# A gate vector moved from VectorE's dot products to TensorE's matrix products, inside the first layer's attention

## The chip, the cores and the metric

The kernel runs on one core of a Trainium2 chip, in one launch. The metric is the device time of the whole kernel in microseconds (us), the median of several runs. A profiled execution gives the trace from which all rows below are read. Times in the trace count from the start of its span.

## The reference, cut to what matters

The model is two blocks of two layers each over 256 tokens of width 1024. Each layer of the first block begins with a vector `mod` that is computed from a conditioning vector `c` and cut into six parts of 1024 numbers:

```python
mod = silu(c) @ w_ada[l] + b_ada[l]                      # w_ada[l]: 1024 x 6144
sh1, sc1, g1, sh2, sc2, g2 = split(mod, 6)
h = rms_norm(x, norm_g[l, 0]) * (1 + sc1) + sh1
...                                                      # h @ w_in, three mixers: 12 softmax heads, 4 linear ones
mix = concat([o_a, o_b, o_c]) @ w_out[l]
x = x + g1 * mix                                         # g1 is the mixer gate
h = rms_norm(x, norm_g[l, 1]) * (1 + sc2) + sh2
x = x + g2 * conv_ffn(h, ...)
```

The change is about `g1` of the first layer: 1024 numbers, each a dot product of `silu(c)` with a column of `w_ada[0]`, plus a bias.

## The kernel before, in words

Activations lie transposed: 1024 features as 8 chunks of 128 partitions, 256 tokens along the free side. All weights come from HBM in units of 512 KB; SyncE (SP) issues their loads in a written-out order into a ring of 8 slots, and waits for a slot to be freed before it issues the next, so that everything behind a waiting load waits too.

The conditioning vectors need no matrix product before: `w_ada` is stored so that a "row" n is a 128 x 1024 tile whose partition p holds the column of `w_ada` for output feature 128n + p. VectorE multiplies the tile by `silu(c)` (the same on all partitions, in `crow`) and sums along the free side, which gives 128 outputs (`do_ada`, L1810; one such operation is called a dot here). There are 48 rows in a layer: 0 to 15 for the first shift and scale, 16 to 23 for `g1`, 24 to 39 for the second shift and scale, 40 to 47 for `g2`. Rows from 16 on pass through four slots of their own; row n is loaded (L679) once the dot of row n - 4 is done (semaphore `ada_used`). Written-out lists spread the dots over stages in which VectorE was thought free: `ADA_UNITS` gives how many come at each step of the attention, `ADA_OUT` how many at each part of the output projection. `mods` (L1818) then adds the bias.

The attention of the first layer has 12 units (a pair of heads by 128 queries) in a software pipeline over steps. At step s TensorE multiplies the scores of unit s, turns the probabilities of unit s - 3 (four transposes, L921), and multiplies the values of unit s - 4 into one of four PSUM banks (a "job" of this unit). Before the last, it multiplies seven times by zeros (`keep_warm`, L776; bf16, 256 columns), whose results are overwritten. VectorE at step s does its dots, then the maximum of the scores of unit s, the reciprocals of unit s - 1 and the copy of the result of unit s - 5 (L1912), which frees its bank for the job two later. ScalarE exponentiates and copies the turned probabilities out of PSUM; GpSimd scales the probabilities (L1751). Everything waits in order on its own engine.

Then comes the output projection: three banks of two tiles each, then two halves (`last_tiles`), with VectorE adding `g1` times each bank to `x` (`residual`, L1842) between dots, ScalarE squaring the new `x` and TensorE summing the squares for the next norm. Of the eight weight units of this projection (20 to 27), SP issues six before rows 20 to 29 of `w_ada`, two between rows 29 and 30, and the next stage's units between the later rows:

```python
ADA_LOADS = {RING + 6: 4, U_IN + 5: 10, U_IN + 7: 4, U_IN + 8: 2, U_IN + 9: 2, U_IN + 10: 2}
ADA_UNITS, ADA_OUT = [[0] * 4 + [1] * 6 + [2] * 2, [0] * NATT], [(5, 5, 4, 0), (0, 0, 0, 0)]
```

Of the kernel before, what the change touches and what calls it, by code (L numbers as in the profile page):

```python
# [30 lines left out]
RING = 8  # L31
ADA_RING = 4
ADA = 6 * DC
N_CMP, CMP_LEN, CMP_STRIDE = 15, 32, 16
NSA_H, REL_BUCKETS, REL_MAX = 16, 32, 128
PH, NK, TOPK = 8, 128, 16
# [26 lines left out]
def columns():  # L63

    at, n = {}, 0
    for l in range(DEPTH):
        for name, k in (("ng1", DC), ("ng2", DC), ("cw0", 2 * FC), ("cw1", 2 * FC), ("cw2", 2 * FC), ("cb", 2 * FC),
                        ("aq", 1), ("ak", 1), ("cq", 1), ("ck", 1), ("bo", 1), ("lb", 4)):
            at[name, l] = n
            n += k  # L70
    for l in range(2 * DEPTH):
        at["bada", l] = n
        n += ADA
    for name, k in (("png", 4 * DC), ("fcw", 12), ("fq", 1), ("fk", 1), ("bf", 1),
                    ("nq", 1), ("nkc_lo", 1), ("nkc_hi", 1), ("nks", 1), ("nkw", 1),
                    ("bgate", 48), ("pos", 2 * CMP_LEN)):
        at[name] = n
        n += k
    return at, n
# [97 lines left out]
def lay_out(x):  # L177
# [37 lines left out]
    put("bgate", np.broadcast_to(g["odd_b_gate_2"][0], (P, 48)))  # L215
    pos = g["odd_cmp_pos_2"][0]
    put("pos", np.concatenate([dup(pos[0].T), dup(pos[1].T)], 1))
    out["params"] = par
    out["consts"] = constants()
    out["mixer_consts"] = mixer_constants()  # L220
# [2 lines left out]
    out["rel"] = np.ascontiguousarray(table[distance_rows()].transpose(0, 2, 1)).reshape(P, NSA_H * T)  # L223
    out["c_rows"] = np.ascontiguousarray(np.stack([np.broadcast_to(g["c"][0], (P, D)), np.broadcast_to(g["c_2"][0], (P, D))], 1))
    out["ada"] = np.stack([w.T.reshape(ADA, P, D) for w in (*g["w_ada"], *g["ada_w_2"])])

    units = []
    for l in range(DEPTH):
# [74 lines left out]
def build(nc, io, out):  # L303
# [7 lines left out]
    with ctx:  # L311
# [310 lines left out]
        ADA_TURNS = [[24] + [2] * FC + [8, 8, 8, 0], [0] + [2] * 16 + [3] * 6 + [6, 6, 6, 0]]  # L622
        ADA_FOX = (9, 18, 23, 29)
        ADA_LOADS = {RING + 6: 4, U_IN + 5: 10, U_IN + 7: 4, U_IN + 8: 2, U_IN + 9: 2, U_IN + 10: 2}
        ADA_UNITS, ADA_OUT = [[0] * 4 + [1] * 6 + [2] * 2, [0] * NATT], [(5, 5, 4, 0), (0, 0, 0, 0)]
        EARLY = 2 * DEPTH * ADA
        assert EARLY - 16 - sum(map(sum, ADA_TURNS)) == 16
        FIRST = CONST["ones"][1]
# [34 lines left out]
        def _(sp):  # L663
# [6 lines left out]
            def load_ada(k):  # L670

                for _ in range(min(k, EARLY - ada_n[0])):
                    n = ada_n[0]
                    if n >= 16 + ADA_RING:
                        sp.wait_ge(sem("ada_used"), n - ADA_RING + 1)
                    elif n >= 16:
                        sp.wait_ge(sem("ada_used"), 16)
                    arrived = sem(f"ada_first{n // 2}") if n < 16 else sem(f"ada_in{n % ADA_RING}")
                    sp.dma_start(ada_slot(n), io["ada"][n // ADA, ada_row(n)]).then_inc(arrived, 16)  # L679
                    ada_n[0] += 1  # L680
# [64 lines left out]
        def _(pe):  # L745
# [27 lines left out]
            def keep_warm(to, n):  # L773

                for _ in range(n):
                    nc.tensor.matmul(to, zero_b[:, 0:P], zero_b, start=True, stop=True)  # L776

            def norm_stat(o):
                b = open_job("norm", o, 0)
# [109 lines left out]
                        mm(out_[:, h, t], kk[side, h, s * P:(s + 1) * P], qq[side, h, t * P:(t + 1) * P],  # L889
                           signal=sem("lev_filled") if h == 3 and t == 1 else None)  # L890

            def attention(name, us, u0, beside={}, warm={}, warm_values=0):
                n, jobs = len(us), 0
                for step in range(n + 4):
                    if step in beside:
# [28 lines left out]
                    if 0 <= step - 4 < n:  # L924
                        u, un = u0 + step - 4, us[step - 4]
                        nc_ = keys_of(un) // P
                        if un.first:
                            j = (*name, jobs)
                            jobs += 1
                            ob = open_job(*j)  # L930
                            keep_warm(ob[:, 0:T], warm_values)
                        pe.wait_ge(*freed("pt", *name, step - 4))
                        if un.pre is not None:
                            mm(ob[:, 0:P], un.pre[0], un.pre[1], True, False)
                        for c in range(nc_):
                            for hh in range(2):
                                side = slice(hh * HD, (hh + 1) * HD)
                                end = hh and c == nc_ - 1
                                mm(ob[side, 0:P], un.v[:, c, side], pt[:, u % 2, hh, c],
                                   un.first and un.pre is None and c == 0, c == nc_ - 1 and un.last,  # L940
                                   None if not end else filled(*j)[0] if un.last else sem("pv_mid"))

            pe.wait_ge(sem("ones_in"), 16)
            for l in range(DEPTH):
# [34 lines left out]
                def outputs_B():  # L979

                    b = open_job("ob", l, 0)
                    for cc in range(2):
                        for t in range(TT):
# [5 lines left out]

                attention(("att", l), units_of(l), l * NATT,   # L990
                          {1: lambda: pe.wait_ge(sem("lev_freed"), NLEV * (l + 1)), 2: outputs_B, NATT: lambda: stat("statB", l, 1, "sqB", l + 1),
                           6: lambda: pe.wait_ge(sem("qkC"), l + 1)}, *WARM_ATT[l])

                mixed = {c: [freed("att", l, 2 * (c if c < 3 else c - 2) + t) for t in range(TT)] for c in (0, 1, 2, 5, 6, 7)}
                mixed[3] = [(sem("mixB"), l + 1)]
# [315 lines left out]
        def _(act):  # L1311
# [3 lines left out]
            def wait(*sv):  # L1315
                act.wait_ge(*sv)
# [212 lines left out]
            wait(sem("c_in"), 16)  # L1529
            seq(A(crow[:, 0], crow[:, 0], ACT.Silu), "c_silu")  # L1530
            wait(sem("params_in"), 16)

            wait(sem("x_in"), 16)
            for l in range(DEPTH):
# [256 lines left out]
        def _(dve):  # L1791
# [3 lines left out]
            def wait(*sv):  # L1795
                dve.wait_ge(*sv)
# [2 lines left out]

            def do_ada(k):  # L1800
                for _ in range(min(k, EARLY - ada_n[0])):
                    n = ada_n[0]
                    if n < 16:
                        wait(sem(f"ada_first{n // 2}"), 32)
                    else:
                        wait(sem(f"ada_in{n % ADA_RING}"), 16 * ((n - 16) // ADA_RING + 1))
                    if n == DEPTH * ADA:
                        wait(sem("c_silu"), 2)
                    l, ch = n // ADA, ada_row(n)
                    seq(V.tensor_tensor_reduce(out=junk, in0=ada_slot(n), in1=crow[:, l // DEPTH], scale=1.0,  # L1810
                                               scalar=0.0, op0=ALU.mult, op1=ALU.add,
                                               accum_out=mod[:, l, ch // DC, ch % DC:ch % DC + 1]), "ada_used")
                    ada_n[0] += 1
# [60 lines left out]
                for c in range(DC):  # L1874
                    scale(1, c, "h_scaled")

            def attention(name, us, u0, projections=None, beside={}):
                n, jobs = len(us), 0
                projections = projections or [0] * n
                for step in range(n + 5):  # L1880
# [27 lines left out]
                    if 0 <= step - 5 < n and us[step - 5].last:  # L1908
                        j = (*name, jobs)
                        jobs += 1  # L1910
                        wait(*filled(*j))
                        seq(V.tensor_copy(us[step - 5].out, bank_of(*j)[:, 0:P]), *freed(*j))  # L1912

            V.memset(epsc[:, :], EPS).then_inc(sem("eps_set"), 1)
# [30 lines left out]
            for l in range(DEPTH):  # L1945
# [100 lines left out]
                def norm_B():  # L2046
# [2 lines left out]
                    seq(V.tensor_tensor(mixT[:, 3:5], oB, gB, ALU.mult), "mixB")  # L2049

                attention(("att", l), units_of(l), l * NATT, ADA_UNITS[l],
                          {0: lambda: None if l == 0 else roots_C(3), 1: lambda: roots_C(0), 2: lambda: roots_C(1), 3: lambda: roots_C(2), 4: norm_C, NATT + 2: lambda: roots_B(0), NATT + 3: lambda: roots_B(1)})
                norm_B()
                if l == 0:
                    mods(0, 2, 3)
                residual(2 * l + 1, ("out", l), l, 2, ADA_OUT[l], None if l else lambda: mods(0, 3, 5))
                for k in range(FC):
                    g = l * FC + k
# [341 lines left out]
```

## Time and profile before

| what | us |
|---|---|
| median of 3 runs (lowest, highest) | 2473.94 (2468.49, 2475.46) |
| profiled execution, its own time | 2471.28 |
| span of its trace | 2469.5 |
| TensorE matmul busy | 2407.2 |
| VectorE busy | 1612.8 |
| ScalarE busy | 847.6 |
| GpSimd busy | 298.9 |

The profiled execution is 2.66 us below the median. Its own time is 1.78 us more than the span, which is what lies around the traced instructions. The stage in question, from the start of the attention to the end of the output projection, is less than 90 us of the span (121 to 209 us).

### The profile page before, as it was taken

Reading aid. Unit: us, or ns where it says so; the run is one execution under the profiler, and the core shown is the slowest. Engines: PE = TensorE matmul, PEld = TensorE weight load, DVE = VectorE, ACT = ScalarE, POOL = GpSimd, SP = SyncE. Lnnn points to the kernel's source line nnn. Section 1 sums busy time; section 2 is a strip of 40 time slices with the busy share of each in tenths; the row PEclk is TensorE's granted clock in tenths of the full one; section 3 lists DMA queues with packets and bytes.
Section 4 is the critical chain, followed back from the end, with each engine's and each line's share of the span. In section 5 each row is a group of like instructions: output and inputs, shape, how many; then the busy total and the mean of one; then the engine's idle time right before and its main releaser. Section 6 shows DMA issues by size and latency. Waiting matters only on the chain.

```text
span 2469.5 us, 46042 instructions
## 1 busy us (share of the span) xinstructions
PE 2407.2 (97%) x17350; PEld 2234.2 (90%) x17350; DVE 1612.8 (65%) x3756; ACT 847.6 (34%) x2183; POOL 298.9 (12%) x386
## 2 busy tenths in 40 slices
PE   7989999999999999999999999999899999999998
PEld 6868889878888987999999999989599999999998
DVE  6886665574666273795888883325639958888634
ACT  2542120443110113223665540022622246655300
POOL 1030110010110001010111121100401101111110
PEclk9999999999999999999999999999999999999999
DMA  8447888314889562699999999954038989999997
GB/s 321 158 166 280 305 291 331 129 59 147 312 302 360 198 245 78 224 413 347 401 408 402 407 405 414 394 193 162 1 129 316 414 325 409 407 396 413 406 413 294
DMA packets 171489, 727.06 MB, mean 294 GB/s; under 512 B 19152, under 2 KB 19664, under 8 KB 146384
## 3 DMA queue, kind: packets, MB, share of 16 engines
q1 hardware_dynamic: 142992, 521.76, 56.4%
q0 software_dynamic: 27648, 201.34, 20.1%
q10 hardware_dynamic: 704, 2.10, 0.4%
q8 instruction: 82, 1.34, 0.2%
q14 instruction: 63, 0.52, 0.1%
HBM read 721.97 MB, written 1.05 MB: 293 GB/s over the span
## 4 chain that ended last, share of the span: by engine, by line
PE 87%; DVE 6%; DMA 3%; ACT 2%; issue 2%; POOL 0%; SPq 0%; DVEq 0%; ACTq 0%
PE banks L749 36%; PE lev L1152 23%; PE banks L1098 21%; DMA ring<-in_peer_u 2%; PE lev L749 2%; PE banks L1079 1%; PE lev L1079 1%; PE banks L865 1%; PE banks L921 1%; DMA extra<-in_ada 1%; DVE arena L1965 1%; DVE arena L2031 0%; ACT arena L1423 0%; DVE arena L1991 0%; DVE arena L1894 0%
## 5 line engine op out<-in xcount | busy, mean ns | idle before, releaser
L749 PE MATMUL banks<-hT,ring 128*128 128x256 f32 (+1 forms) x2832 | 584.5, 367 | 4.8 <-ACT hT L1332 3.2
L1098 PE MATMUL banks<-hT,ring 128*128 128x160 f32 x4096 | 579.4, 301 | 3.6 <-DMA ring<-in_peer_u 3.3
L749 PEld LDWEIGHTS banks<-hT,ring 128*128 128x128 f32 x2832 | 513.1, 190 | 72.5 <-ACT hT L1332 5.0
L1152 PE MATMUL lev<-arena,ring 128*128 x4096 | 576.8, 301 | 0.0
L1098 PEld LDWEIGHTS banks<-hT,ring 128*128 128x128 f32 x4096 | 559.2, 190 | 5.3 <-DMA ring<-in_peer_u 1.9
L1152 PEld LDWEIGHTS lev<-arena,ring 128*128 128x128 f32 x4096 | 559.0, 190 | 0.2
L1781 POOL DMA_INDIRECT arena<-in_peer_rows,keysb x192 | 184.9, 963 | 1131.5 <-DVE consts L2192 675.0
L749 PE MATMUL banks<-arena,ring 128*128 128x256 f32 (+2 forms) x1648 | 284.9, 334 | 0.7 <-DVE arena L2049 0.7
L749 PEld LDWEIGHTS banks<-arena,ring 128*128 128x128 f32 x1648 | 259.1, 192 | 25.4 <-DVE arena L2049 1.1
L2239 DVE SCALAR_TENSOR_TENSOR extra<-consts,chT 128x192 bf16<-128x192 f32 x640 | 223.8, 409 | 17.8 <-ACT arena L1471 17.6
L2204 DVE CUSTOM_DVE_ANT_0 arena<-arena 128x1024 f32<-128x1024 f32 x64 | 78.2, 1222 | 165.2 <-DMA arena<-in_peer_rows,keysb 165.1
L2192 DVE SCALAR_TENSOR_TENSOR consts<-arena,extra,consts 128x1024 f32<-128x1024 f32 x128 | 164.1, 1282 | 6.4 <-ACT extra L1482 6.4
L2204 DVE CUSTOM_DVE_ANT_0 arena<-arena,consts 128x1024 f32<-128x1024 f32 x128 | 155.4, 1214 | 0.3
L1810 DVE CUSTOM_DVE_ANT_0 arena<-arena 128x1024 f32<-128x1024 f32 x104 | 130.1, 1251 | 35.1 <-DMA arena<-in_ada 31.5
L1471 ACT ACTIVATE arena<-banks 128x320 f32<-128x320 f32 x128 | 55.9, 437 | 276.2 <-PE banks L1098 255.0
L1491 ACT ACTIVATE std<-consts,chT 128x128 bf16<-128x128 f32 x320 | 102.0, 389 | 76.4 <-PE banks L1079 60.0
L1480 ACT ACTIVATE extra<-extra 128x1 f32<-128x1 f32 x192 | 37.2, 194 | 264.5 <-DVE extra L2204 264.5
L1491 ACT ACTIVATE rstd<-consts,chT 128x128 bf16<-128x128 f32 x320 | 102.0, 389 | 73.3 <-PE banks L1079 54.5
L1618 ACT ACTIVATE arena<-banks,params 128x256 f32<-128x256 f32 x88 | 44.8, 559 | 237.0 <-PE banks L749 237.0
L1810 DVE CUSTOM_DVE_ANT_0 arena<-extra,arena 128x1024 f32<-128x1024 f32 x88 | 109.0, 1238 | 21.6 <-DMA extra<-in_ada 18.9
L1751 POOL TENSOR_SCALAR arena<-arena,rinv 128x256 f32<-128x256 f32 (+1 forms) x128 | 64.1, 513 | 417.8 <-DVE rinv L1904 258.2
L2065 DVE SCALAR_TENSOR_TENSOR arena<-banks,params,arena 128x255 f32<-128x255 f32 x88 | 42.5, 483 | 101.0 <-ACT arena L1618 99.4
(286 smaller groups left out, 2284.3 us busy)
## 6 DMA issues: line engine op xcount, KB each, us to landing
ring<-in_peer_u SPq DMA_DIRECT2D x256, 512.0 KB
ring<-in_peer_v SPq DMA_DIRECT2D x256, 512.0 KB
ring<-in_stream_first SPq DMA_DIRECT2D x188, 512.0 KB
arena<-in_ada SPq DMA_DIRECT2D x104, 512.0 KB, 5.4
extra<-in_ada SPq DMA_DIRECT2D x88, 512.0 KB, 5.3
ring<-in_stream_nsa SPq DMA_DIRECT2D x45, 512.0 KB
ring<-in_stream_fox SPq DMA_DIRECT2D x41, 512.0 KB
arena<-in_peer_rows,keysb POOLq DMA_INDIRECT x192
```

The source lines that it names most:

```text
L749: ins = nc.tensor.matmul(o, lhsT, rhs, start=start, stop=stop, **kw)
L1079: ins = nc.tensor.matmul(gate_banks[half][k % 2][:, t * 256:t * 256 + HALF], hot_r[:, k % 2, t], hot_c[:, k % 2, t, i], start=i == 0, stop ...
L1098: ins = nc.tensor.matmul(banks[k // 2 % 4][:, (k % 2) * ND:(k % 2 + 1) * ND], ring[:, u % RING, c], hT[:, c, NS:T], start=c == 0, stop=c = ...
L1152: ins = nc.tensor.matmul(lev[c // 4][:, (c % 4) * T + NS:(c % 4 + 1) * T], ring[:, u % RING, c], a[:, bass.ds(g, 1), k], start=False, stop ...
L1471: A(acts_g[:, g, 2 * k:2 * k + 2], banks[k][:, 0:2 * ND].rearrange("p (a t) -> p a t", a=2), ACT.Gelu_apprx_tanh).then_inc(sem("act_freed" ...
L1491: A(dist[q % 2][:, t], iota, ACT.Abs, bias=chT[:, 0, 4 * q + t:4 * q + t + 1])\
L1751: G.tensor_scalar(x, x, rinv[:, u % 4, hh:hh + 1], 1.0, ALU.mult, ALU.mult).then_inc(sem("probs_ready"), 1)
L1781: G.indirect_dma_start(out=rows[:, n % ROWS], out_offset=None, in_=io["peer_rows"], in_offset=bass.IndirectOffsetOnAxis(ap=eid[:, k:k + 1] ...
L1810: seq(V.tensor_tensor_reduce(out=junk, in0=ada_slot(n), in1=crow[:, l // DEPTH], scale=1.0, scalar=0.0, op0=ALU.mult, op1=ALU.add, accum_o ...
L2192: V.scalar_tensor_tensor(out=y, in0=rows[:, n % ROWS, D:2 * D], scalar=row_act[:, k:k + 1], in1=y, op0=ALU.mult, op1=ALU.add).then_inc(sem ...
L2204: V.tensor_tensor_reduce(out=u, in0=u, in1=xn[i], scale=1.0, scalar=0.0, op0=ALU.mult, op1=ALU.add, accum_out=row_act[:, k:k + 1]).then_in ...
L2239: ins = V.scalar_tensor_tensor(out=hot_c[:, q % 2, t], in0=iota[:, half * HALF:(half + 1) * HALF].unsqueeze(1).broadcast_to([P, PARTS, HALF]),
```

## The change

Rows 16 to 23 are no longer dots. They are stored so that each 128 x 128 block of a row's tile is a weight for TensorE (input features on the partitions, output features along the free side). `silu(c)` is also kept as `ccol`, one column per chunk and each column twice, computed by a small operation of ScalarE at the start; it adds 16 columns to the loaded parameters. In the jobs of units 0 to 5 the seven products by zeros are replaced by `gate_products`: two rows in jobs 0 and 1, one in jobs 2 to 5, each row 8 matrix products (f32, 128 x 128 weights, 2 moving columns) that accumulate into two spare columns of the job's bank. VectorE adds the bias to each row's column, before the copy of this job, with one operation on 128 x 1. The jobs of units 6 to 11 keep their zeros.

VectorE's dots in the attention go from 10 (one at steps 4 to 9, two at 10 and 11) to 4 (one at steps 8 to 11), those in the output projection from 14 to 12; the call of `mods` for the gate is gone. SP's order of loads is the same, but rows 20 to 27 now wait for TensorE's use of rows 16 to 23, and rows 28 on for the dots of rows 24 on.

```diff
+GATE_ROWS = range(2 * DC, 3 * DC)
...
+    put("ccol", np.repeat(ch(g["c"][0]), 2, 1))
...
+    for n in GATE_ROWS:
+        out["ada"][0, n] = g["w_ada"][0][:, n * P:(n + 1) * P].reshape(DC, P, P).transpose(1, 0, 2).reshape(P, D)
...
-        ADA_UNITS, ADA_OUT = [[0] * 4 + [1] * 6 + [2] * 2, [0] * NATT], [(5, 5, 4, 0), (0, 0, 0, 0)]
+        ADA_UNITS, ADA_OUT = [[0] * 8 + [1] * 4, [0] * NATT], [(4, 4, 4, 0), (0, 0, 0, 0)]
+        GATE_JOBS = [{0: (16, 17), 1: (18, 19), 2: (20,), 3: (21,), 4: (22,), 5: (23,)}, {}]
+        ccol = col("ccol", None, 0, 2 * DC).rearrange("p (c a) -> p c a", a=2)
...
-                    if n >= 16 + ADA_RING:
-                        sp.wait_ge(sem("ada_used"), n - ADA_RING + 1)
+                    if n >= 24 + ADA_RING:
+                        sp.wait_ge(sem("ada_used"), n - ADA_RING + 1 - DC)
+                    elif n >= 16 + ADA_RING:
+                        sp.wait_ge(sem("gate_rows"), n - ADA_RING - 16 + 1)
...
+            def gate_products(b, rows):
+
+                for i, n in enumerate(rows):
+                    if n == GATE_ROWS[0]:
+                        pe.wait_ge(sem("c_col"), 1)
+                    pe.wait_ge(sem(f"ada_in{n % ADA_RING}"), 16 * ((n - 16) // ADA_RING + 1))
+                    for c in range(DC):
+                        mm(b[:, T + 2 * i:T + 2 * i + 2], ada_slot(n)[:, c * P:(c + 1) * P], ccol[:, c], c == 0, c == DC - 1,
+                           sem("gate_rows") if c == DC - 1 else None)
...
-                            keep_warm(ob[:, 0:T], warm_values)
+                            if jobs - 1 in gates:
+                                gate_products(ob, gates[jobs - 1])
+                            else:
+                                keep_warm(ob[:, 0:T], warm_values)
...
+            A(ccol, ccol, ACT.Silu).then_inc(sem("c_col"), 1)
...
+                    if ada_n[0] == GATE_ROWS[0]:
+                        ada_n[0] += DC
...
+                        for i, r in enumerate(gates.get(jobs - 1, ())):
+                            r -= GATE_ROWS[0]
+                            seq(V.tensor_tensor(mod[:, 0, 2, r:r + 1], bank_of(*j)[:, T + 2 * i:T + 2 * i + 1],
+                                                col("bada", 0, GATE_ROWS[0] + r), ALU.add))
...
-                if l == 0:
-                    mods(0, 2, 3)
```

## Rows read from the trace of the kernel before

**Rows 1.** The page: the chain that ended last by engine, and one group.
```profile
PE 87%; DVE 6%; DMA 3%; ACT 2%; issue 2%; POOL 0%; SPq 0%; DVEq 0%; ACTq 0%
...
L1480 ACT ACTIVATE extra<-extra 128x1 f32<-128x1 f32 x192 | 37.2, 194 | 264.5 <-DVE extra L2204 264.5
```

**Rows 2.** Timeline of VectorE, attention: start us, us, instruction, [idle before].
```profile
149.91 1.28 DVE L1810 CUSTOM_DVE_ANT_0 arena<-arena 128x1024 f32<-128x1024 f32 x1
...
152.69 1.28 DVE L1810 CUSTOM_DVE_ANT_0 arena<-extra,arena 128x1024 f32<-128x1024 f32 x1
...
154.02 1.37 DVE L1810 CUSTOM_DVE_ANT_0 arena<-extra,arena 128x1024 f32<-128x1024 f32 x1
```

**Rows 3.** Timeline of TensorE, attention; an f32 product is two passes, counted singly.
```profile
134.32 0.93 PE L776 MATMUL banks<-zero 128*128 128x256 bf16 x7
...
143.55 0.70 PE L749 MATMUL lev<-arena 64*128 64x256 f32 x4
144.18 0.66 PE L921 MATMUL banks<-consts,arena 128*128 128x128 f32 x4
144.68 0.93 PE L776 MATMUL banks<-zero 128*128 128x256 bf16 x7
145.53 0.66 PE L749 MATMUL banks<-arena 128*64 128x128 f32 x8
146.12 0.70 PE L749 MATMUL lev<-arena 64*128 64x256 f32 x4
...
156.92 0.94 PE L776 MATMUL banks<-zero 128*128 128x256 bf16 x7 [1.46 <-DVE arena L1912]
...
161.21 0.63 PE L921 MATMUL banks<-consts,arena 128*128 128x128 f32 x4 [1.71 <-DVE arena L1912]
```

**Rows 4.** Timeline of TensorE, output projection.
```profile
169.22 24.56 PE L749 MATMUL banks<-arena,ring 128*128 128x256 f32 x128
...
196.80 0.75 PE L749 MATMUL banks<-arena,consts 128*128 128x128 f32 x4 [2.13 <-ACT arena L1323]
197.35 3.58 PE L749 MATMUL banks<-arena,ring 128*128 128x128 f32 x16
...
207.22 1.95 PE L749 MATMUL banks<-hT,ring 128*128 128x128 f32 x16
```

**Rows 5.** Timeline of TensorE, the last sums of the experts, 32 columns moving.
```profile
1616.18 1.87 PE L1166 MATMUL lev<-folds,arena 128*128 128x32 f32 x16
1617.88 1.69 PE L776 MATMUL banks<-zero 128*128 128x256 bf16 x14
```

**Rows 6.** TensorE by line and form: xcount, busy us, mean ns, idle before.
```profile
L749 PE MATMUL banks<-arena 128*128 128x30 f32 x32 | 3.7, 271 | 0.0
...
L1138 PE MATMUL lev<-zero 128*128 128x2 bf16 x8 | 0.5, 163 | 1.2 <-ACT arena L1471 1.2
```

**Rows 7.** Windows: stretch, length, then busy time by engine, TensorE's granted clock, DMA.
```profile
124.00:126.00 2.00, 1.37 (x12) 0.70 (x8) 1.93 (x3) 0.36 (x1) 0.00 (x0) 0.92 0.03 8
126.00:128.00 2.00, 2.00 (x13) 1.25 (x14) 1.95 (x2) 0.66 (x4) 0.00 (x0) 0.50 0.00 0
...
198.00:200.00 2.00, 2.00 (x11) 2.00 (x11) 0.00 (x0) 0.00 (x0) 0.00 (x0) 0.50 0.00 0
...
1714.00:1716.00 2.00, 2.00 (x22) 2.00 (x20) 2.00 (x1) 0.00 (x0) 0.00 (x0) 1.00 0.00 0
```

**Rows 8.** Timeline of VectorE, output projection.
```profile
171.25 0.17 DVE L1818 TENSOR_TENSOR mod<-mod,params 128x8 f32<-128x8 f32 x1
...
192.62 1.23 DVE L1810 CUSTOM_DVE_ANT_0 arena<-extra,arena 128x1024 f32<-128x1024 f32 x1 [1.35 <-DMA extra<-in_ada]
...
195.15 0.88 DVE L1842 SCALAR_TENSOR_TENSOR xT<-banks,mod,xT 128x256 f32<-128x256 f32 x2
```

**Rows 9.** Loads of `w_ada` rows, 120 to 200 us, from issue to landing.
```profile
DMA to landing us min/median/max: 3.0/4.6/6.8
```

**Rows 10.** SP's queue in the same stage: issues merged by line.
```profile
172.71 1.60 SPq L679 DMA_DIRECT2D extra<-in_ada  x2
```

More of the change, by code:

```diff
@@ L75, in columns @@
                     ("nq", 1), ("nkc_lo", 1), ("nkc_hi", 1), ("nks", 1), ("nkw", 1),
-                    ("bgate", 48), ("pos", 2 * CMP_LEN)):
+                    ("bgate", 48), ("pos", 2 * CMP_LEN), ("ccol", 2 * DC)):
         at[name] = n
@@ L890, in level, with attention @@
                            signal=sem("lev_filled") if h == 3 and t == 1 else None)
-            def attention(name, us, u0, beside={}, warm={}, warm_values=0):
+            def attention(name, us, u0, beside={}, warm={}, warm_values=0, gates={}):
                 n, jobs = len(us), 0
@@ L991, in _ @@
                           {1: lambda: pe.wait_ge(sem("lev_freed"), NLEV * (l + 1)), 2: outputs_B, NATT: lambda: stat("statB", l, 1, "sqB", l + 1),
-                           6: lambda: pe.wait_ge(sem("qkC"), l + 1)}, *WARM_ATT[l])
+                           6: lambda: pe.wait_ge(sem("qkC"), l + 1)}, *WARM_ATT[l], GATE_JOBS[l])
                 mixed = {c: [freed("att", l, 2 * (c if c < 3 else c - 2) + t) for t in range(TT)] for c in (0, 1, 2, 5, 6, 7)}
@@ L1875, in residual, with attention @@
                     scale(1, c, "h_scaled")
-            def attention(name, us, u0, projections=None, beside={}):
+            def attention(name, us, u0, projections=None, beside={}, gates={}):
                 n, jobs = len(us), 0
@@ L2051, in _ @@
                 attention(("att", l), units_of(l), l * NATT, ADA_UNITS[l],
-                          {0: lambda: None if l == 0 else roots_C(3), 1: lambda: roots_C(0), 2: lambda: roots_C(1), 3: lambda: roots_C(2), 4: norm_C, NATT + 2: lambda: roots_B(0), NATT + 3: lambda: roots_B(1)})
+                          {0: lambda: None if l == 0 else roots_C(3), 1: lambda: roots_C(0), 2: lambda: roots_C(1), 3: lambda: roots_C(2), 4: norm_C, NATT + 2: lambda: roots_B(0), NATT + 3: lambda: roots_B(1)}, GATE_JOBS[l])
                 norm_B()
-                if l == 0:
-                    mods(0, 2, 3)
                 residual(2 * l + 1, ("out", l), l, 2, ADA_OUT[l], None if l else lambda: mods(0, 3, 5))
```

## The prediction

> **What bounds the kernel now.** I read the page's chain first: 87% of the span is TensorE, 6% VectorE [rows 1]. So a dot that leaves VectorE is worth something only where VectorE is on the chain, and a product that TensorE gains costs its whole time wherever TensorE is. I therefore went to the attention of the first layer, in the timelines of both engines. VectorE runs there without a gap: with one dot a step takes 2.78 us (149.91 to 152.69), of which the dot is 1.28 [rows 2]; a second dot adds 1.33 (152.69 to 154.02), which makes about 4.1. TensorE, when nothing holds it, needs 2.57 us for a step (143.55 to 146.12): scores 0.63, transposes 0.50, seven zeros 0.85, values 0.59 [rows 3]. In the steps with one dot the two are nearly equal. In the two steps with two dots TensorE waits, 1.46 and 1.71 us [rows 3], and these two waits are about all that ten dots cost here. The output projection starts at 169.22 [rows 4]. I call this moment T0.
>
> Behind T0 TensorE works through the projection, then stands still for 2.13 us at 194.7 to 196.8, waiting for ScalarE's squares of the new x [rows 4]. These wait for VectorE's add at 195.15, which came late because the dots before it waited for their rows from HBM (1.35 us for the last pair) [rows 8]. After this wait the clock was granted at half: 0.50 in 198 to 200 us [rows 7]. Sixteen passes took 3.58 us there, and the like sixteen 1.95 us at full clock [rows 4]: 1.63 us lost.
>
> **What the gate costs on TensorE.** No product with 2 columns and f32 weights is in the trace. The nearest have 32 columns: sixteen passes, the number of one row (8 products of two passes), from 1616.18 to 1617.88, 1.70 us, 0.106 a pass [rows 5]. With 30 columns it is 3.7 us for 32, 0.116 a pass [rows 6]. Since 32 columns are no faster than 128 (1.95 less the overlap of the last), the weights set the pace, and I take 1.70 us for a row. Below, the bound is the bf16 product with 2 columns, 0.5 us for eight, 0.062 each [rows 6], or 1.0 us a row; but f32 weights are twice the bytes, and I stay at 1.70. Above it is 1.86 with the 30-column figure. The seven zeros that go cost 0.85. So blocks with two rows gain 2.55 us, those with one 0.85.
>
> The Trainium skill (TensorE: Matmul & The Clock Gate, section Back-to-back issue gap) gives about 25 ns from start to start for products of 1 to 64 columns; by that a row would be 0.4 us and cheaper than the zeros. The 32-column row has four times this, and I go by the row.
>
> **T0 at full clock.** A step now is scores, transposes and values, 1.72 us, and the products. Job 0 begins at 134.32 as before [rows 3]; two steps of 5.12 and four of 3.42 bring job 6 to 158.2. From its zeros on: 1.44 for zeros and values of job 6, 2.57 for step 11, then 1.94, 1.94, 1.94 and 1.44 for steps 12 to 15, 0.9 for the statistic of the linear heads in step 12 (two passes of 512 columns, each twice a pass of 256 columns at 24.56 us for 128 passes of which 32 are half as wide [rows 4], 0.22), and an estimate of 0.5 for the wait for its square root, together 12.7. T0 is 170.9, or 1.7 later than before. In place of a kernel held by two double dots stands one held by 13.6 us of gate products (8 x 1.70) where 5.1 us of zeros were.
>
> Is VectorE hidden then? With one dot its step is 2.78, against 3.42 of TensorE in steps 8 and 9 and 2.57 in 10 and 11; it starts these with steps 4 to 7 without dots behind it, so it follows TensorE's scores by about 2 us at the end, and the copy of job 5 is there when the zeros of job 7 need it. The eight bias adds are 0.2 each by the like operation on 128 x 8 [rows 8], 1.6 us spread over steps in which VectorE waits; without this cover they would cost that much. The bias call of 0.2 that goes was off TensorE's path too.
>
> SP's queue: row 20 is issued once row 16 is used, at about 136, and a load lands in 3.0 us at least, 4.6 at the median [rows 9]; job 2 wants it at 144.6. Rows 24 to 27 follow the single blocks, from about 146.3 in steps of 3.42, and land 3.0 later, at 149.3, when VectorE asks; even the median 4.6 delays a dot by 1.6 us at a place with 2 us to spare. Behind them in the queue stand rows 28 and 29 and weight units 26 and 27, which are wanted only at the end of the projection.
>
> **The projection.** VectorE has 12 dots, not 14, and SP issues rows 30 and 31 at once behind unit 27, where row 30 stood at 172.71, T0 + 3.5 [rows 10], since the dots that they wait for are done. Each later row is issued about 2.5 us nearer to T0. Chained through, the last dot ends near T0 + 20.5, and the third bank is only there at T0 + 21 (96 passes of 0.22). So the add is done by T0 + 22, not at 196.0, T0 + 26.8; TensorE wants the squares at 194.7, T0 + 25.4. The wait goes (-2.1) and with it the half clock behind it (-1.6). What is late next is TensorE itself. The small silu of `ccol` adds about 0.2 at the start, where ScalarE leads to the first norm; such operations take 194 ns [rows 1].
>
> At full clock all this gives 1.7 + 0.2 - 2.1 - 1.6 = -1.8 us.
>
> **The clock.** The zeros stand there for the clock, and what replaces them moves 2 columns a pass where they moved 256. Before the fall at 125.7 TensorE was busy 1.37 of 2 us, partly on half of its rows (64 of 128), and then had 0.50 [rows 7]. The only long stretch of thin products, 3.7 us with 30 columns [rows 6], kept 1.00 in 1714 to 1716 [rows 7]; but it has 15 times the columns and dense work on both sides. Neither row settles what 3.4 us of 2-column products do. I take the clock to fall: a half-clock stretch like the one in [rows 4] loses 1.63 us. The gates of job 1 at half clock take 6.8 us, about twice the 3.58 of that row, and I add one more among jobs 2 to 5, whose steps are half gates: 3 x 1.63 = 4.9.
>
> The Trainium skill (the same page, section Why this matters for your kernels) asks only that TensorE have no long idle gap between bursts. The gates leave none, so by this rule the clock stays. The fall at 125.7 came with TensorE idle for only 0.63 of the 2 us around it [rows 7], so the trace doesn't bear it out fully.
>
> The forecast is -1.8 + 4.9 = +3.1 us: 2474.3 on the profiled 2471.28, and 2477 on the median 2473.94.
>
> **Rivals.**
> A. The clock stays at 1.00: a busy engine is enough. For it speaks 1714 to 1716. The sum is -1.8, 2472.1.
> B. The clock is at half through most of the six blocks. Each single step then has 3.4 us of gates and up to 3.4 of other work (1.72 doubled), and the clock falls again as soon as it has come back. With ten stretches it is -1.8 + 16.3 = +14.5, 2488.4. It is slower beyond what can be measured from the sixth stretch on (-1.8 + 6 x 1.63 = 8.0). Against it: the four single steps have dense work in between, and such work gave the clock back in the projection, where the sixteen passes from 207.22 run at full pace again [rows 4].
> C. The wait in the projection stays, since ten rows still come through there and full bandwidth is shared with the weight units. Then the 3.7 us aren't recovered: +6.8, 2480.7. Against it: some 3 us of slack.
> D. The 2-column passes run at 0.062. A row is 1.0 and costs 0.15 more than the zeros; the steps are 3.7 twice and 2.7 four times, T0 is near 165.4, or about 166 (an estimate) with VectorE's four dots, and the sum is about -3.2 + 0.2 - 3.7 = -6.7, 2467.2. Against it: [rows 5].
> That the dots don't leave VectorE is not possible by the diff.
>
> **How the numbers follow.** Chances: forecast (one to five stretches) 0.45, A 0.28, B 0.12, C 0.08, D 0.07. Within 0.3% (7.4 us, about what a measurement of this kernel tells from no change) lie A, C and nearly all of the forecast, and half of D: 0.79. Slower holds B and 0.03 of forecast and C: 0.15. Faster holds the rest of D and what I have missed: 0.06. The range is 2467 to 2487: D's edge below, all of the forecast's own 2473 to 2480, A and C, and half of B; under 0.2 is left out.
>
> **What would show it.** Right: gate rows of 16 passes with 1.70 us from start to start; TensorE without waits in steps 4 to 11; T0 between 171 and 177; two to four stretches with a granted clock of 0.50 between 135 and 165; no idle time before the norm's sums at T0 + 25 and 1.00 behind it. Wrong: a row under 1.2 or over 2 us; TensorE waiting for rows 20 to 23 or for VectorE's copies; a wait of 2 us left in the projection; the clock at 1.00 throughout, or at half to 170.

## The result, and the profile after

The changed kernel takes 2483.28 us (median of 9 runs, 2478.01 to 2488.80) against 2471.94 us for the kernel before (9 runs): a ratio of 1.0047, with a 95% interval of 1.0035 to 1.0058, or about 11 us more. The forecast was 2477 in a range of 2467 to 2487. The time lies in the range and on the side of the forecast, but at more than three times its +3.1, and in the class "slower by over 0.3%", which had a chance of 0.15. It is above the 2473 to 2480 of the forecast's own case: the range held it because it took in half of rival B.

The profiled execution took 2488.80 us, the longest of the nine, with a span of 2486.9 against 2469.5. The timeline of TensorE in the attention of the first layer, where [rows 3] stood:

```profile
133.27 3.63 PE L757 MATMUL banks<-params,arena 128*128 128x2 f32 x32
136.83 0.66 PE L757 MATMUL banks<-arena 128*64 128x128 f32 x8
...
139.41 6.83 PE L757 MATMUL banks<-params,extra 128*128 128x2 f32 x32
146.17 1.12 PE L757 MATMUL banks<-arena 128*64 128x128 f32 x8
147.22 1.23 PE L757 MATMUL lev<-arena 64*128 64x256 f32 x4
148.37 1.11 PE L939 MATMUL banks<-consts,arena 128*128 128x128 f32 x4
149.28 3.41 PE L757 MATMUL banks<-params,arena 128*128 128x2 f32 x16
152.62 1.12 PE L757 MATMUL banks<-arena 128*64 128x128 f32 x8
```

The first two rows of the gate take 3.56 us together (133.27 to 136.83). Behind them the values still run at full pace (0.59 to the next start), but from the scores at 137.42 on everything takes about twice as long: the two rows of job 1 take 6.76 us, one row 3.34, and the scores, transposes and values around them are as slow. A single step takes 6.45 us (149.28 to the like place at 155.73) where 3.42 was reckoned. The windows say why (stretch, length, busy us of TensorE, its weight loads, VectorE, ScalarE, GpSimd, then TensorE's granted clock, the DMA engines' share and GB/s):

```profile
134.00:137.00 3.00, 3.00 (x29) 2.98 (x31) 2.41 (x4) 2.79 (x9) 2.31 (x3) 1.00 0.25 76
138.00:178.00 40.00, 40.00 (x201) 33.40 (x199) 14.05 (x49) 9.42 (x31) 9.74 (x12) 0.50 0.36 123
178.00:180.00 2.00, 2.00 (x15) 1.36 (x15) 0.97 (x5) 0.52 (x3) 0.00 (x0) 0.88 0.46 186
```

For 40 us on end TensorE was busy without a break and had half its clock (1.2 GHz). It came back only after the first job that has zeros again (175.09). The kernel before had 1.00 from 130 to 190 us; around this stage it fell twice, each time for some 3 us: before 130 us, and behind the wait in the projection [rows 7]. VectorE is busy 14 of the 40 us: it now waits for scores, 8.09 us before the maximum of unit 6.

```profile
148.59 0.42 DVE L1918 CUSTOM_DVE_ANT_0 arena<-lev,arena 128x256 f32<-128x256 f32 x1 [8.09 <-PE lev L757]
```

The projection, where [rows 4] and [rows 8] stood, on TensorE and then on VectorE:

```profile
188.86 24.56 PE L757 MATMUL banks<-arena,ring 128*128 128x256 f32 x128
213.25 1.06 PE L757 MATMUL banks<-arena,consts 128*128 128x128 f32 x8
214.57 0.71 PE L757 MATMUL banks<-arena,consts 128*128 128x128 f32 x4 [0.26 <-ACT arena L1344]
215.12 1.95 PE L757 MATMUL banks<-arena,ring 128*128 128x128 f32 x16
```

```profile
194.71 1.23 DVE L1834 CUSTOM_DVE_ANT_0 arena<-extra,arena 128x1024 f32<-128x1024 f32 x1 [1.33 <-DMA extra<-in_ada]
...
212.92 0.88 DVE L1866 SCALAR_TENSOR_TENSOR xT<-banks,mod,xT 128x256 f32<-128x256 f32 x2
```

The wait of 2.13 us is 0.26 now, and the sixteen passes behind it take 1.95 us where they took 3.58. Two lengths can be worked out from such timelines for every kernel: A, from the first product of job 0 to T0 (the start of the projection), and B, from T0 to the place in the next stage where TensorE waits 0.48 us for ScalarE's hT. Before, A is 34.90 us (134.32 to 169.22) and B is 40.43 (to 209.65). After, A is 55.59 and B is 36.93. Their sum grew by 17.2 us, and the span by 17.4: all of the loss is here, 20.7 lost in the attention and 3.5 given back in the projection.

The nine executions differ in how long the clock is at half. The one of 2478.01 us has a mean granted clock of 0.991 over a span of 2475.9, the profiled one 0.987 over 2486.9: worked out, 45 and 65 us at half clock in the whole kernel, against 25 us at the 0.995 of the kernel before, each to within some 2.5 us, since the mean clock is given to 0.001. The profiled execution is the worst case of the nine, not a middle one.

### The profile page after: what moved, and what is told of

Read it like the earlier page. It is cut to its first block, busy times and chain, and to the rows that moved or that the text cites. A ratio compares the mean times of both kernels' runs of the same rounds, so it can differ in the third digit from the quotient of the medians.

```text
span 2486.9 us, 46204 instructions
## 1 busy us (share of the span) xinstructions
PE 2432.2 (98%) x17436; PEld 2258.6 (91%) x17436; DVE 1603.1 (64%) x3747; ACT 848.1 (34%) x2184; POOL 296.6 (12%) x386
## 4 chain that ended last, share of the span: by engine, by line
PE 88%; DVE 6%; DMA 3%; ACT 2%; issue 1%; POOL 0%; SPq 0%; DVEq 0%; ACTq 0%
PE banks L757 37%; PE lev L1173 23%; PE banks L1119 21%; PE lev L757 2%; DMA ring<-in_peer_u 2%; PE banks L1100 1%; PE lev L1100 1%; PE banks L883 1%; PE banks L939 1%; DMA extra<-in_ada 1%; DVE arena L1993 1%; DVE arena L2059 0%; ACT arena L1444 0%; PE banks L784 0%; DVE arena L2019 0%
## 5 line engine op out<-in xcount | busy, mean ns | idle before, releaser
L2230 DVE CUSTOM_DVE_ANT_0 arena<-arena 128x1024 f32<-128x1024 f32 x64 | 78.2, 1222 | 166.7 <-DMA arena<-in_peer_rows,keysb 166.7
L1834 DVE CUSTOM_DVE_ANT_0 arena<-arena 128x1024 f32<-128x1024 f32 x100 | 124.7, 1247 | 37.8 <-DMA arena<-in_ada 34.3
L1834 DVE CUSTOM_DVE_ANT_0 arena<-extra,arena 128x1024 f32<-128x1024 f32 x84 | 103.8, 1236 | 22.1 <-DMA extra<-in_ada 19.6
```

The source lines that it names most:

```text
L2230: V.tensor_tensor_reduce(out=u, in0=u, in1=xn[i], scale=1.0, scalar=0.0, op0=ALU.mult, op1=ALU.add, accum_out=row_act[:, k:k + 1]).then_in ...
```

## The experiments

In the text below "over" and "under" are against the kernel before on the same chip. In the edits, what is not shown is as in the changed kernel unless it says otherwise.

**1. As many columns as the weights' pace gives for nothing: 128.**

```diff
-    mm(b[:, T + 2 * i:T + 2 * i + 2], ada_slot(n)[:, c * P:(c + 1) * P], ccol[:, c], ...
+    mm(b[:, T + 128 * i:T + 128 * i + 128], ada_slot(n)[:, c * P:(c + 1) * P], ccol[:, c, 0:1].broadcast_to([P, 128]), ...
```

VectorE's bias add reads column 128i of the spare ones instead of 2i.

> The changed kernel with 128 moving columns in each gate product instead of 2 (the same column 128 times), nothing else. Theory: the half clock of 137 to 178 us comes from what the gate products stream, 2 columns a pass, while the weights alone set their pace. Then a row still takes about 1.8 us, TensorE's clock stays at 1.00 from 134 us to the projection, the projection starts near 171 instead of 188.9, and the time is 1 to 3 us under the kernel before (ratio 0.999). Rival: it is the chain of long weight-bound stretches itself, whatever it streams. Then the clock is 0.50 here too and the time is that of the changed kernel, ratio 1.004.

Measured: 2469.17 us against 2473.33, ratio 0.9984 (0.9975 to 0.9992), 4.2 us under. The windows of the attention and of the projection, columns as above:

```profile
134.00:172.00 38.00, 37.53 (x335) 29.98 (x336) 23.49 (x69) 20.34 (x55) 10.28 (x20) 1.00 0.45 153
172.00:210.00 38.00, 37.32 (x237) 34.10 (x236) 26.57 (x57) 9.91 (x24) 0.00 (x0) 1.00 0.72 278
```

and two of its rows in the timeline, with the start of the projection:

```profile
134.35 3.74 PE L757 MATMUL banks<-params,arena 128*128 128x128 f32 x32
138.01 0.66 PE L757 MATMUL banks<-arena 128*64 128x128 f32 x8
...
145.11 1.95 PE L757 MATMUL banks<-params,arena 128*128 128x128 f32 x16
146.99 0.66 PE L757 MATMUL banks<-arena 128*64 128x128 f32 x8
...
172.42 24.56 PE L757 MATMUL banks<-arena,ring 128*128 128x256 f32 x128
```

The same products with 64 times the columns cost 3.66 us for two rows instead of 3.56, the clock is 1.00 throughout, and A is 38.07. Nothing else differs from the changed kernel but the column that the bias add reads, so the half clock there is caused by how little the products stream, not by their number, their weights or any wait that the change moved. The rival falls.

**2. 32 columns.** The same edit with 32 in place of 128.

> The changed kernel with 32 moving columns in each gate product. If streaming matters, this stands between 2 and 128: a row takes 1.7 us at full clock, and half-clock stretches are fewer than in the changed kernel; time 0 to 8 us over the kernel before. If streaming doesn't matter, it is the changed kernel's time, 11 us over.

Measured: 2483.93 us, ratio 1.0042 (1.0027 to 1.0056), 10.6 us over: no better than 2 columns. The profiled execution had the whole block at half clock:

```profile
134.00:137.00 3.00, 3.00 (x28) 2.99 (x27) 2.55 (x5) 2.79 (x8) 2.14 (x3) 1.00 0.18 40
138.00:178.00 40.00, 40.00 (x199) 33.21 (x195) 14.05 (x49) 9.61 (x31) 9.74 (x12) 0.50 0.36 119
```

I had expected something in between. Taken alone the run would have fitted the rival, that streaming doesn't matter; beside experiment 1 it says that this kernel loses the clock with 32 columns as it does with 2.

**3. Thin products in the kernel before.** In the kernel before, the zeros of jobs 0 to 5 give way to as many products of 2 columns as the change has; their results are overwritten. The dots stay.

```diff
-    keep_warm(ob[:, 0:T], warm_values)
+    if name == ("att", 0) and jobs - 1 < 6:
+        for c in range(16 if jobs - 1 < 2 else 8):
+            nc.tensor.matmul(ob[:, T:T + 2], ident, ones[:, 0:2], start=True, stop=True)
+    else:
+        keep_warm(ob[:, 0:T], warm_values)
```

> The kernel before, with all its dots on VectorE, where only the seven products by zeros of jobs 0 to 5 are replaced by as many thin ones as the change has (16 f32 products of 2 columns in jobs 0 and 1, 8 in jobs 2 to 5; their results are overwritten). Theory: the clock falls to 0.50 as in the changed kernel, and the loss is at least the changed kernel's: 11 to 20 us over the kernel before, since the wait in the projection stays or shrinks only with the later start. Rival: the fall is due to something else that the change moved (waits for rows, the copies on VectorE); then the clock stays at 1.00 and the time is 2 to 5 us over.

Measured: 2483.87 us, ratio 1.0047 (1.0030 to 1.0065), 10.5 us over. This is the changed kernel's loss, without its change of the dots. In the profiled execution the clock came back twice on the way, at about 156 us, only to be lost again before 160, and at about 166, both times with nothing but thin rows, scores, transposes and values since the fall:

```profile
139.00:156.00 17.00, 17.00 (x86) 15.00 (x85) 6.73 (x18) 4.34 (x16) 5.75 (x6) 0.50 0.38 123
156.00:160.00 4.00, 4.00 (x37) 3.48 (x35) 2.67 (x9) 1.63 (x6) 1.90 (x2) 0.93 0.19 38
160.00:166.00 6.00, 6.00 (x31) 5.00 (x32) 2.54 (x9) 1.50 (x6) 1.89 (x2) 0.50 0.45 152
```

```profile
156.15 1.89 PE L933 MATMUL banks<-consts 128*128 128x2 f32 x16
...
159.70 3.42 PE L933 MATMUL banks<-consts 128*128 128x2 f32 x16
...
166.16 1.99 PE L933 MATMUL banks<-consts 128*128 128x2 f32 x16
```

A is 49.23 (134.23 to 183.46), and TensorE still waits 2.86 us in the projection. What lets the clock come back in one execution and not in another I haven't tested; the same kind of difference stands between the nine executions of the changed kernel.

**4. Only the dots go.** The gate products are left out and seven zeros stand in each job again; the gate is not computed. This is what eight dots less are worth, with nothing in their place.

```diff
-    for c in range(DC):
-        mm(b[:, T + 2 * i:T + 2 * i + 2], ada_slot(n)[:, c * P:(c + 1) * P], ccol[:, c], ..., sem("gate_rows") if c == DC - 1 else None)
+    k = 7 if len(rows) == 1 else (4, 3)[i]
+    keep_warm(b[:, 0:T], k - 1)
+    mm(b[:, 0:T], zero_b[:, 0:P], zero_b, signal=sem("gate_rows"))
```

> The changed kernel without its gate products: the seven products by zeros stand in jobs 0 to 5 again, and the gate is not computed (the bias is added to zeros). This is what taking eight dots off VectorE is worth alone. Theory: the two waits of 1.5 and 1.7 us in the attention go and T0 comes 3 to 4 us earlier, the wait of 2.1 us in the projection and its half clock go: 5 to 8 us under the kernel before. Rival: VectorE or the loads of the rows hold the attention anyway; then 0 to 3 us under.

Measured: 2465.34 us, ratio 0.9969 (0.9958 to 0.9981), 8.0 us under, at the upper end of what was expected. A is 31.59 (133.13 to 164.72), 3.3 less than before, and B is 36.62, 3.8 less. TensorE has no wait before the sums of the norm:

```profile
189.12 1.71 PE L757 MATMUL banks<-arena,consts 128*128 128x128 f32 x12
190.67 1.95 PE L757 MATMUL banks<-arena,ring 128*128 128x128 f32 x16
```

**5. A filler behind the thin products.** The changed kernel with 2 columns, and the seven zeros kept behind the gate products of jobs 0 to 5.

> The changed kernel (2 columns) with the seven products by zeros kept behind the gate products of jobs 0 to 5. Theory: dense work between thin stretches brings the clock back sooner: two to five half-clock stretches around jobs 0 and 1 instead of twelve, at the price of 5.1 us of zeros: 2 to 8 us over the kernel before. Rival: the stretches of thin products are too long for any filler behind them; then the clock stays down through the six jobs and the zeros double in price too: 18 us or more over.

Measured: 2481.02 us, ratio 1.0036 (1.0021 to 1.0051), 9.2 us over, a little more than expected. The clock was at half in one stretch, from 139.4 us, behind the first double block, through the second, to about 153:

```profile
138.00:144.00 6.00, 6.00 (x37) 4.91 (x37) 1.46 (x5) 2.76 (x10) 1.67 (x4) 0.62 0.46 159
144.00:150.00 6.00, 6.00 (x30) 5.28 (x31) 0.00 (x0) 0.00 (x0) 0.00 (x0) 0.50 0.35 111
150.00:156.00 6.00, 6.00 (x47) 4.70 (x45) 1.63 (x8) 1.57 (x5) 0.93 (x2) 0.74 0.17 66
156.00:162.00 6.00, 6.00 (x57) 4.78 (x53) 3.46 (x12) 1.80 (x6) 1.97 (x2) 1.00 0.51 175
```

```profile
134.47 3.63 PE L757 MATMUL banks<-params,arena 128*128 128x2 f32 x32
137.96 0.92 PE L784 MATMUL banks<-zero 128*128 128x256 bf16 x7
...
141.46 6.83 PE L757 MATMUL banks<-params,extra 128*128 128x2 f32 x32
...
157.25 1.84 PE L757 MATMUL banks<-params,arena 128*128 128x2 f32 x16
158.95 0.92 PE L784 MATMUL banks<-zero 128*128 128x256 bf16 x7
```

The first double block itself ran at full clock (3.49 us), and so did the single blocks of jobs 3 to 5, one row of 1.70 us and 0.85 us of zeros. In this execution the zeros kept the clock behind one thin row, and not behind two. They are a dear way to do it: A is 48.15.

**6. Four rows instead of eight.** Rows 16 to 19 go to TensorE, one in each of jobs 0 to 3, with 128 columns; rows 20 to 23 stay dots.

```diff
-GATE_ROWS = range(2 * DC, 3 * DC)
+GATE_ROWS = range(2 * DC, 2 * DC + 4)
-        ADA_UNITS, ADA_OUT = [[0] * 8 + [1] * 4, [0] * NATT], [(4, 4, 4, 0), (0, 0, 0, 0)]
-        GATE_JOBS = [{0: (16, 17), 1: (18, 19), 2: (20,), 3: (21,), 4: (22,), 5: (23,)}, {}]
+        ADA_UNITS, ADA_OUT = [[0] * 5 + [1] * 7, [0] * NATT], [(4, 5, 4, 0), (0, 0, 0, 0)]
+        GATE_JOBS = [{0: (16,), 1: (17,), 2: (18,), 3: (19,)}, {}]
...
+                if l == 0:
+                    seq(V.tensor_tensor(mod[:, 0, 2, 4:8], mod[:, 0, 2, 4:8], col("bada", 0, 20, 4), ALU.add))
```

> Only rows 16 to 19 go to TensorE, one in each of jobs 0 to 3, with 128 moving columns; the other four gate rows stay dots (seven dots in the attention, one at each of steps 5 to 11, and 13 in the projection). Theory: the double dots were what the dots cost, and the first two rows hide in waits that TensorE has in jobs 0 and 1 anyway. T0 comes 2 to 3 us before 169.2, the clock stays at 1.00, most of the projection's wait goes: 3 to 7 us under the kernel before, and 0 to 3 us under the run with eight wide rows. Rival: the wait in the projection comes back with its 13th dot; then it is level with the eight wide rows or above.

Measured: 2470.18 us against 2471.82, ratio 0.9992 (0.9984 to 1.0001), 1.6 us under: a miss. The projection's wait did come back in part (1.19 us), but most was lost in the attention, by a new wait. VectorE:

```profile
138.88 1.23 DVE L1834 CUSTOM_DVE_ANT_0 arena<-arena 128x1024 f32<-128x1024 f32 x1 [2.02 <-DMA arena<-in_ada]
142.84 1.22 DVE L1834 CUSTOM_DVE_ANT_0 arena<-arena 128x1024 f32<-128x1024 f32 x1 [1.28 <-DMA arena<-in_ada]
146.98 1.22 DVE L1834 CUSTOM_DVE_ANT_0 arena<-extra,arena 128x1024 f32<-128x1024 f32 x1 [1.25 <-DMA extra<-in_ada]
151.72 1.23 DVE L1834 CUSTOM_DVE_ANT_0 arena<-extra,arena 128x1024 f32<-128x1024 f32 x1 [1.85 <-DMA extra<-in_ada]
```

and TensorE behind it, with a granted clock of 0.54 from 155 to 158 us, after this wait:

```profile
154.66 1.17 PE L784 MATMUL banks<-zero 128*128 128x256 bf16 x7 [2.00 <-DVE arena L1940]
```

A dot of step s wants the slot that the row of step s - 1 has only just left, and the load between takes longer than that. It is the wait that I had worked out for the change itself, and not for my own variant.

**7. 64 columns, twice.** As experiment 1, with 64.

> The changed kernel with 64 moving columns in each gate product, between 32 (all six blocks at half clock) and 128 (none). At full clock the price of a row is 1.7 us at either width. If the clock falls here, the time is 11 us over the kernel before as with 32; if it stays, 2 to 5 us under as with 128, perhaps a little better, since a pass of 64 columns is not slower. It may do both in different executions.

> The eight rows with 64 moving columns again, on the same chip as the run beside it, to compare the two. It gave 4.3 us under the kernel before; 3 to 6 us under is expected again, with no granted clock of 0.50 in the attention.

Measured: 2467.49 us, ratio 0.9982 (0.9973 to 0.9991), and in the second run 2469.13, ratio 0.9986 (0.9977 to 0.9995): 4.3 and 3.7 us under. The clock is 1.00 from 134 to 180 us in both profiles:

```profile
134.00:171.00 37.00, 36.53 (x330) 29.05 (x329) 22.54 (x66) 20.43 (x56) 10.24 (x20) 1.00 0.46 157
```

A is 37.81 and B 36.92. Between 32 and 64 columns the same kernel goes from 10.6 us over to 4 us under.

**8. Four thin rows.** As experiment 6, with 2 columns.

> As the run with four rows, one in each of jobs 0 to 3, but with 2 moving columns. Theory: single thin rows of 1.7 us between dense work lower the clock less surely than double ones; 0 to 4 half-clock stretches, so between 5 us under the kernel before (clock stays) and 3 us over (clock down through four jobs).

Measured: 2470.46 us, ratio 0.9993 (0.9984 to 1.0002), 1.4 us under. Its ten executions lie between 2467.33 and 2476.19; the profiled one is the longest, with 0.50 from 138 to 160 us and A of 44.13. A single thin row per step puts the clock at risk as well: here it was lost at about 137, behind the first.

**9. Four rows, earlier.** Experiment 6 with 64 columns, two rows in job 0, one in job 1 and one in job 2, so that each slot is free a step sooner.

```diff
-        GATE_JOBS = [{0: (16,), 1: (17,), 2: (18,), 3: (19,)}, {}]
+        GATE_JOBS = [{0: (16, 17), 1: (18,), 2: (19,)}, {}]
```

> The four rows again (16 to 19 on TensorE), with 64 moving columns, but taken earlier: two in job 0, one in job 1, one in job 2, so that each slot is free a step sooner for the row whose dot VectorE wants. In the last trace of four rows VectorE waited 2.0, 1.3, 1.3 and 1.9 us for these rows and TensorE 2.0 us behind it. Theory: those waits go, T0 comes 1.5 to 2.5 us before that of the kernel before, and the time is 4 to 7 us under it, level with the eight rows of 64 columns or up to 2 us better. Rival: the loads still land late, or the 13 dots of the projection bring its wait back; then it stays at 1 to 3 us under.

Measured: 2466.69 us against 2472.86, ratio 0.9974 (0.9964 to 0.9985), 6.2 us under, beside 3.7 under for eight rows of 64 columns on the same chip. This version is faster than the kernel before and the changed one. Two waits of VectorE for rows are left (1.98 and 0.93 us), and TensorE has none behind them:

```profile
139.02 1.22 DVE L1834 CUSTOM_DVE_ANT_0 arena<-arena 128x1024 f32<-128x1024 f32 x1 [1.98 <-DMA arena<-in_ada]
142.81 1.23 DVE L1834 CUSTOM_DVE_ANT_0 arena<-arena 128x1024 f32<-128x1024 f32 x1 [0.93 <-DMA arena<-in_ada]
145.73 1.25 DVE L1834 CUSTOM_DVE_ANT_0 arena<-extra,arena 128x1024 f32<-128x1024 f32 x1
```

```profile
167.91 24.56 PE L757 MATMUL banks<-arena,ring 128*128 128x256 f32 x128
```

A is 34.12 (133.79 to 167.91), 0.8 less than before though TensorE has four rows more to do, and B is 37.37. Two things differ from experiment 6, the jobs and the width. The width alone, with eight rows, made 0.1 to 0.3 us in A (37.81 and 37.97 with 64 columns, 38.07 with 128), and A is 3.4 shorter here.

The lengths A and B of one profiled execution each, the span of this execution, and the difference of the medians, in us:

| kernel | A | B | A + B against before | span against before | medians against before |
|---|---|---|---|---|---|
| before | 34.90 | 40.43 | | | |
| changed, 2 columns | 55.59 | 36.93 | +17.2 | +17.4 | +11.3 |
| 32 columns | 55.76 | 36.96 | +17.4 | +13.7 | +10.6 |
| thin products in before | 49.23 | 39.54 | +13.4 | +11.5 | +10.5 |
| 2 columns and zeros | 48.15 | 36.78 | +9.6 | +9.5 | +9.2 |
| 64 columns | 37.81 | 36.92 | -0.6 | -4.8 | -4.3 |
| 64 columns again | 37.97 | 37.22 | -0.1 | -2.7 | -3.7 |
| 128 columns | 38.07 | 36.83 | -0.4 | +0.5 | -4.2 |
| four rows, 128 columns | 37.47 | 37.86 | 0.0 | -1.5 | -1.6 |
| four rows, 2 columns | 44.13 | 38.43 | +7.2 | +4.9 | -1.4 |
| four rows early, 64 columns | 34.12 | 37.37 | -3.8 | -4.6 | -6.2 |
| dots left out | 31.59 | 36.62 | -7.1 | -9.5 | -8.0 |

One profile is too coarse for a few us. In these twelve, job 0 begins between 133.1 and 134.5 us and what follows B takes 2256.8 to 2261.1 us (134.3 and 2259.9 before), though no edit changes the work there but for the small operation on `ccol`. The profiled execution also lies off its median: 2.8 us above it with 128 columns, 5.7 above it with four rows of 2 columns, 3.3 below it with the dots left out, and that of before (2471.28) is below all medians of its runs (2471.82 to 2473.94). So the losses of 9 us and more are read in the stage, while for the wide columns the gain of about 4 us is shown by the medians, and how much of it lies in the stage stays open.

## Why the prediction was right or wrong

**What bounds the kernel: right.** The dots were worth the two double ones in the attention and the late add in the projection. With the dots alone left out, A shrinks by 3.3 us, where the two waits were 1.46 and 1.71, and B by 3.8, where 2.1 and 1.6 were named. In the attention the sum agrees better than its parts. The prediction's "these two waits are about all that ten dots cost here" passed over two waits of the kernel before, for ScalarE's copies of the turned probabilities in jobs 0 and 1:

```profile
136.37 0.66 PE L749 MATMUL banks<-arena 128*64 128x128 f32 x8 [1.12 <-ACT arena L1434]
140.39 0.66 PE L749 MATMUL banks<-arena 128*64 128x128 f32 x8 [1.38 <-ACT arena L1434]
```

With the dots left out the first stays (1.11) and the second is 0.15, while four small waits for VectorE's copies, 0.43, 0.20, 0.20 and 0.26, are left in the place of the two long ones. With gate products in jobs 0 and 1 both waits for ScalarE are gone: the products fill them. These 2.5 us, beside the 3.2 of the two double dots, help to explain why A grows by 2.9 to 3.2 us only, with 64 or 128 columns, where the gate products take 9.4 to 9.7 us more than the zeros.

**The price of a gate row: a little low.** 1.70 us was taken; two rows took 3.56 at full clock, 1.78 each, and a single row with zeros behind it 1.70 (experiment 5). The 2, 32 and 64 columns with f32 weights all took 3.56 to 3.62 for two rows (3.62 with 64 in experiment 9, 133.79 to 137.41), so the 32-column row of the trace was the right neighbour. The Trainium skill's figure of about 25 ns for small products (TensorE: Matmul & The Clock Gate, section Back-to-back issue gap) makes an estimate of 0.4 us a row. No run here came near it.

**T0 at full clock: low by a little over 1 us.** From job 0 to T0 36.6 was worked out (134.32 to 170.9). Measured with the clock at 1.00: 37.81 with 64 columns, 38.07 with 128. Most of it is the rows' price: from job 0 to the zeros of job 6 it took 24.81 (64 columns) and 25.13 (128) where 23.9 was worked out, and from there to T0 13.00 and 12.94 where 12.7 was. The 0.2 us for `ccol` at the start can't be seen: job 0 begins earlier in the changed kernel's profile (133.27) than before.

**VectorE and the loads in the attention: right.** TensorE waits neither for rows 20 to 23 nor for VectorE's copies in steps 4 to 11. At half clock this was easy; the runs with 64 and 128 columns show it at full clock, where VectorE waited 0.31 to 0.81 us for rows, within the 2 us that it had to spare.

**The projection: right in sum, wrong in its slack.** 3.7 us were to come back and 3.5 did. But "some 3 us of slack" was not there: VectorE's add was done at 213.80, T0 + 24.9, and not by T0 + 22, since rows 30 and 31, issued at once as forecast, still landed 1.33 and 0.95 us after VectorE wanted them, and two of the last part came late too, by 1.17 and 0.98. TensorE waited 0.26. The slack was what spoke against rival C, and it was smaller than that: with 12 dots the wait was 0 to 0.55 us in all runs, with the 13 dots of the four-row versions 0.70, 1.19 and 1.75, and with 14 dots 2.13 and 2.86 (the kernel before and experiment 3).

**The clock: right that it falls, wrong by a factor in how long.** The step that failed is the term "3 x 1.63 = 4.9", with its sentence "and I add one more among jobs 2 to 5". Job 1 was taken rightly (6.8 reckoned, 6.76 measured), but in jobs 2 to 5 the clock was not down for one stretch but throughout: in the profiled execution 40 us on end at 0.50, as rival B has it. "At half to 170" stands in the prediction's own list of what would show it wrong. The attention lost 20.7 us, where 1.7 + 4.9 = 6.6 were forecast; 3.2 of this remain at full clock (128 columns), so the clock's part is 17.5 in this execution and, by the medians, 15.5 us (11.3 over with 2 columns, 4.2 under with 128), where the forecast had 4.9 and rival B 16.3. Against the profiled execution of before the profiled one is 17.5 us longer, beyond rival B's 14.5; the medians' 11.3 lies between B and the forecast. It is the 15.5 of the clock less the 4.2 of the rest, for which -1.8 was worked out; with the -1.8 it would have been 13.7, which on the 2473.94 of the forecast is just outside the range. That the time fell into it is in part luck. I gave B 0.12 because "the four single steps have dense work in between": over that work (1.72 us of scores, transposes and values in a step) the clock did not come back in the profiled execution, and nothing in the trace of before had shown such a mixture.

Two slips are in the sums: 3.1 on 2471.28 is 2474.4, not 2474.3; and the five chances make 1.00 already, so the share within 0.3% is 0.81 to 0.82 by them, not 0.79, and the share of faster is 0.035.

By the Trainium skill's advice to leave TensorE no long idle gap (TensorE: Matmul & The Clock Gate, section Why this matters for your kernels) the clock would have stayed here. The trace disagrees: 40.00 of 40 us busy at 0.50. A's chance of 0.28 rested on that reading and on the stretch with 30 columns at 1714 us, which had dense work on both sides; with 32 columns in these six blocks the clock fell.

## What to carry to other kernels

Products that fill a gap for the clock and products that compute are not interchangeable by their time: what stands in for a filler has to stream as well. Where f32 weights set the pace, a product of 2 columns costs nearly as much as one of 64 (two rows 3.56 us against 3.62), so repeat the column until the clock holds, and look at the granted clock of exactly that stretch, not at busy time. Move only as much off an engine as its waits are worth (here the double dots), and follow the slots of what stays: a load that waits for the new user of a slot can be late for the next.

## What the runs showed of the hardware that I had not expected

TensorE can be busy for 40 us without a gap and be granted half its clock the whole time, when about half of that time goes to f32 products of 2 or 32 moving columns, each with fresh 128 x 128 weights. With 64 or 128 columns in the same places it had 1.00. The weight loads slow down with the clock too: in the changed kernel one of the gate's loads took 333 ns on average between 138 and 178 us, and 192 between 133 and 137. A row of 16 passes with 2 columns took 3.34 us against 1.78, so a thin product pays for the lost clock almost in full although it hardly streams.

What brings the clock back is not settled. Over ordinary work between thin rows it did not come back in the profiled executions with 2 and 32 columns and with four thin rows, but twice in that of experiment 3. With seven bf16 products of 256 columns more in each block it came back and stayed (experiment 5), in the one execution that was profiled.
